# Three tiles of the delta rule under way at once, with each score piece's product, rectification and addition placed slots apart

## What is computed

```
h = rms_norm(x); proj = h @ w_in          # q, k, v, indexer q/k/w, delta-rule q/k/v/z, b, a
# A: sparse attention. For each query t and each key s (chunk-causal):
iscore[t, s] = sum_h w[t, h] * relu(q_idx[t, h] . k_idx[s])      # 8 indexer heads
keep the 256 best keys of every query, softmax attention over them
# B: gated delta rule, chunks of 64, per head
a = I + strict_tril((k * beta) k^T * decay)
u, w = solve(a, [v * beta, k * beta * exp(gc)])
v_new = u - w @ state
o = (q * exp(gc)) @ state + att @ v_new
state = state * g_last + k_tail^T @ v_new
x = x + concat(o_a, rms_norm(o) * silu(z)) @ w_out
x = x + square(relu(rms_norm(x) @ w_ff1)) @ w_ff2 ; rms_norm(x)
```

## Time and profile before

| | us |
|---|---|
| median of 3 runs (lowest, highest) | 4432.31 (4430.19, 4437.88) |
| profiled execution | 4433.13 |
| its span, first to last instruction | 4431.3 |
| mean granted clock of TensorE | 0.894 |

### The profile page before, as it was taken

The page is one execution under the profiler, slowest core; times in us unless marked ns, Lnnn a source line. Parts: engine busy times, 40 slices in busy tenths (PEclk is TensorE's granted clock), DMA queues, the critical chain, the costliest instruction groups (busy, mean ns, idle before and its releaser), DMA issues.

```text
span 4431.3 us, 47714 instructions
## 1 busy us (share of the span) xinstructions
PE 3629.1 (82%) x16994; PEld 2930.3 (66%) x16994; DVE 2057.7 (46%) x3590; ACT 2188.2 (49%) x3674; POOL 1257.9 (28%) x648
## 2 busy tenths in 40 slices
PE   3899997567676666646689998899988899998998
PEld 2688885456555544534567776778776788876886
DVE  3101330466766444435364564756655757543222
ACT  3112222365564333333569768687777684443322
POOL 0110111322322322113234342333332333333442
PEclk7899998787888777776889999999999999999999
DMA  2111123210101111023333334333333333333332
GB/s 72 65 71 66 71 76 95 57 36 22 47 24 38 43 45 30 23 65 103 91 93 108 107 111 128 95 106 118 101 116 116 108 110 106 94 108 105 95 96 75
DMA packets 294561, 358.65 MB, mean 81 GB/s; under 512 B 23361, under 2 KB 234177, under 8 KB 290369
## 3 DMA queue, kind: packets, MB, share of 16 engines
q1 hardware_dynamic: 290464, 327.68, 25.5%
q10 hardware_dynamic: 3888, 28.31, 1.5%
HBM read 297.80 MB, written 58.10 MB: 80 GB/s over the span
## 4 chain that ended last, share of the span: by engine, by line
PE 26%; ACT 14%; DVE 7%; issue 5%; POOL 2%; SPq 1%; DMA 1%; ACTq 0%; DVEq 0%; POOLq 0%
PE m_ps L1823 7%; PE m_ps L1825 7%; PE m_ps L1824 7%; ACT m_junk L1536 6%; ACT m_wh L1593 2%; PE m_ps L1917 1%; PE m_ps L1903 1%; ACT m_prob L1620 1%; ACT m_verdict L1538 1%; ACT m_trial L1542 1%; ACT m_phi L1609 1%; PE m_ps L1888 1%; PE m_ps L1889 1%; PE m_ps L1866 1%; ACT m_rl L1552 1%
## 5 line engine op out<-in xcount | busy, mean ns | idle before, releaser
L1481 POOL TENSOR_TENSOR m_wl<-m_raw,m_wh 128x1024 fp32r<-128x1024 f32 x288 | 716.0, 2486 | 1414.5 <-ACT m_wh L1593 1414.5
L1823 PE MATMUL m_ps<-m_ah,m_wh 128*128 128x512 f32 x1280 | 537.8, 420 | 69.1 <-DVE m_al L1682 40.4
L1825 PE MATMUL m_ps<-m_ah,m_wl 128*128 128x512 f32 x1280 | 512.2, 400 | 0.0
L1824 PE MATMUL m_ps<-m_al,m_wh 128*128 128x512 f32 x1280 | 512.0, 400 | 0.0
L1823 PE MATMUL m_ps<-m_th,m_wh 128*128 128x512 f32 x1024 | 428.4, 418 | 41.6 <-DVE m_tl L1662 25.1
L1825 PE MATMUL m_ps<-m_th,m_wl 128*128 128x512 f32 x1024 | 406.4, 397 | 0.0
L1824 PE MATMUL m_ps<-m_tl,m_wh 128*128 128x512 f32 x1024 | 405.3, 396 | 0.0
L1536 ACT ACTIVATE m_junk<-m_sc,m_trial 128x1152 int8<-128x1152 f32 (+7 forms) x248 | 401.6, 1619 | 1.3
L656 PE MATMUL i_ps<-i_keys,i_qhi 128*128 128x512 f32 (+3 forms) x304 | 171.5, 564 | 264.2 <-ACT i_relu L834 250.9
L1593 ACT ACTIVATE m_wh<-m_raw 128x1024 fp32r<-128x1024 f32 x288 | 302.6, 1051 | 126.8 <-PE m_ps L1825 122.0
L250 PE MATMUL ps<-xh,wh 128*128 128x512 f32 x864 | 337.0, 390 | 12.4 <-POOL wl L126 12.4
(11 more groups left out here) (292 smaller groups left out, 7487.8 us busy)
## 6 DMA issues: line engine op xcount, KB each, us to landing
m_raw<-w_units SPq DMA_DIRECT2D x288, 512.0 KB, 3.7
m_vals<-valsT SPq DMA_DIRECT2D x256, 128.0 KB, 3.7
projT<-stage ACTq DMA_DIRECT2D x15, 1024.0 KB, 3.9
wraw<-w_proj SPq DMA_DIRECT2D x28, 512.0 KB, 3.6
projT<-work ACTq DMA_DIRECT2D x12, 1024.0 KB, 3.9
g_qkvz<-projT SPq DMA_DIRECT2D x16, 768.0 KB, 6.2
work<-xT SPq DMA_DIRECT2D x8, 1024.0 KB, 5.7
i_rot<-projT SPq DMA_DIRECT2D x32, 256.0 KB, 4.5
```

Source lines behind the costliest of these rows:

```text
L1481: nc.gpsimd.tensor_tensor(wl[:, n % 3, :], raw[:, n % 2, :], wh[:, n % 3, :].bitcast(fp32), ALU.subtract).then_inc(w_lo, 1)
L1823: nc.tensor.matmul(dst, hi, rh, start=first, stop=False)
L1824: nc.tensor.matmul(dst, hi, r_low, start=False, stop=False)
L1825: return nc.tensor.matmul(dst, lo, rh, start=False, stop=last)
```

## The change

The back is divided into a middle (b0 to b7) and a tail (b8 to b12). In round r the tail is for tile r - 2, the middle for tile r - 1, and the front for tile r: 18 rounds in place of 16 and a front of its own. The steps of the three parts alternate in a new `ROUND`. Each part has its own counting semaphores, `Z` has two buffers, and each part has two PSUM banks (the middle loses its third, the front too, the tail gets its own two), for which PE waits at some places where a bank's reader comes late. A piece's product is now placed at least one slot behind the rectification whose bank it needs, its rectification at least one slot behind the addition whose buffer it needs, and its addition at least one slot behind its rectification. The diff, cut:

```diff
-ROUND = "b0 f0 b1 f1 b2 f2 b3 f3 b4 b5 f4 b6 f5 b7 f6 b8 b9 f7 b10 b11 b12".split()
+ROUND = "b8 b0 b9 b1 b10 f0 b2 b11 f1 b3 b12 f2 b4 f3 b5 f4 b6 f5 b7 f6 f7".split()
+FRONT, MID, TAIL = range(3)
+PART = {"f%d" % i: FRONT for i in range(8)} | {"b%d" % i: MID if i < 8 else TAIL for i in range(13)}
...
-        end = STAGES * NT
+        end = STAGES * (NT + 2)
...
-                slot = dve(slot, ("acc", j, h, x), 760)
+                slot = dve(slot, None, 760)
...
+                score_slot.append(max(ready, slot - 2, relu_slot[n - 2] + 1 if n >= 2 else 0))
+                relu_slot.append(max(score_slot[n], acc_slot[n - RELUS] + 1 if n >= RELUS else 0))
+                slot = max(slot, relu_slot[n] + 1)
                 acc_slot.append(slot)
-                relu_slot.append(max(ready, slot - 3, acc_slot[n - RELUS] if n >= RELUS else 0))
-                score_slot.append(max(ready, relu_slot[n] - 2, relu_slot[n - 2] if n >= 2 else 0))
...
-        BANK = {n: i % 3 for i, n in enumerate("ssq ssk gb kk att NT atT kT vT n2 m2".split())}
-        BANK |= {n: 3 + i % 3 for i, n in enumerate(
-            "n4 m4 Y1 n8 Y2 Y3 Dinv E F Z1 E2 F2 Z2 E4 Z3 wT vnew out state oss".split())}
+        BANK = {n: i % 2 for i, n in enumerate("ssq ssk gb kk att NT atT kT vT n2 m2".split())}
+        BANK |= {n: 2 + i % 2 for i, n in enumerate("n4 m4 Y1 n8 Y2 Y3 Dinv E F Z1 E2 F2 Z2 E4 Z3".split())}
+        BANK |= {"wT": 4, "vnew": 5, "out": 4, "state": 5, "oss": 5}
...
-            for s in [s for s in ROUND if s[0] == "f"]:
-                front(0, s)
-            for t in range(NT):
+            for r in range(NT + 2):
                 for m, s in enumerate(ROUND):
-                    selection(t, m)
-                    if s[0] == "b":
-                        back(t, s)
-                    elif t + 1 < NT:
-                        front(t + 1, s)
+                    selection(r, m)
+                    t = r - PART[s]
+                    if 0 <= t < NT:
+                        (front if PART[s] == FRONT else back)(t, s)
...
+                if s == "f1":
                     po("G")
+                    ac("ln")
                     over_features("gb", B("G")).then_inc(done_f, 1)
...
                     transposes("atT", B("at")).then_inc(done_f, 1)
-                    transposes("kT", qk[:, 1, :, :]).then_inc(done_f, 1)
                 if s == "f6":
                     dv("LT")
+                    transposes("kT", qk[:, 1, :, :]).then_inc(done_f, 1)
+                    ac("attT")
                     transposes("vT", qkvz[:, t % 2, 2, :, :]).then_inc(done_f, 1)
                 if s == "f7":
                     po("n")
-                    ac("attT")
+                    dv("kbe")
                     heads(0, "n2", B("m"), B("n"))
-                    dv("kbe")
+                    dv("vb")
                     heads(0, "m2", B("n"), B("m"))
...
                     po("Y")
+                    ac("n4")
                     heads(1, "Y1", B("n2"), B("Y"))
...
                     heads(1, "E2", B("F"), B("E"))
+                    dv("Z1")
                     heads(1, "F2", B("E"), B("F"))
```

More of the change, by code:

```diff
@@ L314, in dve @@
             ahead[0] += cost
-            self.put("dve", slot, part)
+            if part:
+                self.put("dve", slot, part)
             return slot
@@ L464, in deltanet_and_selection @@
         stored = [sem(f"g_stored{u}") for u in range(2)]
-        done = {e: [sem(f"g_{e}_{part}") for part in ("front", "back")] for e in ("pe", "dve", "act", "pool")}
+        done = {e: [sem(f"g_{e}_{part}") for part in ("front", "mid", "tail")] for e in ("pe", "dve", "act", "pool")}
         z_in = [sem(f"g_z_in{u}") for u in range(2)]
@@ L551, in selection @@
                         sp.dma_start(biasT[j, :, 0:(j + 1) * P], ties[:, 0:(j + 1) * P]).then_inc(bias_stored, 16)
-            for t in range(NT):
-                if t + 2 < NT:
-                    waits(sp, t, 0)[0]("vT")
-                    waits(sp, t, 0)[1]("qk")
-                    load_tile(t + 2, 0, 3, load)
-                for m in range(STAGES):
-                    selection(t, m)
-                waits(sp, t, 1)[3]("out")
-                sp.dma_start(mixT[4:8, :, tokens(t)].rearrange("c p s -> p c s"), out_b[:, t % 2, :, :]).then_inc(stored[t % 2], 16)
-                if t + 2 < NT:
-                    load_tile(t + 2, 3, 4, z_in)
+            for r in range(NT + 2):
+                if 1 <= r < NT - 1:
+                    waits(sp, r - 1, FRONT)[0]("vT")
+                    waits(sp, r - 1, FRONT)[1]("qk")
+                    load_tile(r + 1, 0, 3, load)
+                for m in range(STAGES):
+                    selection(r, m)
+                t = r - TAIL
+                if t >= 0:
+                    waits(sp, t, TAIL)[3]("out")
+                    sp.dma_start(mixT[4:8, :, tokens(t)].rearrange("c p s -> p c s"), out_b[:, t % 2, :, :]).then_inc(stored[t % 2], 16)
+                    if t + 2 < NT:
+                        load_tile(t + 2, 3, 4, z_in)
             for u in range(2):
@@ L616, in back @@
             def back(t, s):
-                pe, dv, ac, po = waits(pool, t, 1)
-                step = lambda ins: ins.then_inc(done["pool"][1], 1)
+                pe, dv, ac, po = waits(pool, t, PART[s])
+                step = lambda ins: ins.then_inc(done["pool"][PART[s]], 1)
                 if s == "b0":
@@ L873, in back @@
                     pe("out")
+                    if t:
+                        waits(act, t - 1, TAIL)[3]("out")
                     step(nc.scalar.activation(B("osq"), bank("out"), ACT.Square))
```

79 lines of the change are left out of this document (45 added, 34 removed).

## The result

The changed kernel takes 4211.76 us in the median of 4 runs (4209.04 to 4215.33); the kernel before, run beside it on the same chip, takes 4434.94 (4 runs, 4430.19 to 4437.88). The ratio is 0.9503, with a 95% interval of 0.9491 to 0.9515: 223 us less. Forecast were 4223, between 4110 and 4370.

The account below looks back on a forecast made before the run. The second stage was taken as bound by hand-offs, same-slot waits making each slot a sum. Round 0, rounds 1 to 10, 11 to 16 and 17 gave 68 + 498 + 390 + 42 = 998 us against 1207: 4223 us, range 4110 to 4370.

Parts of the forecast that it names:

- rounds 0 and 1: Second stage's start: round 0 with first front, key rotation and first pieces at 68 us, then one early round at 47.
- rounds 2 to 10: Early rounds, DVE fullest: 47 us each, plus 10 for rounds 3 and 7 and 8 for waits on rotated queries.
- round 17: Last round, no front or middle, 30 pieces: 21 slots of two additions and a hand-off, 42 us.
- A late round: Rounds 11 to 16: PE busy 54 us plus 11 of stalls, 65 us each; bounds 57 and 76.
- busy time times granted clock takes the clock out: Step costing PE's late-round work at full clock: 46.8 us, then 54 at clock 0.87.
- What PE still stands for: Late-round PE stalls: rectification wait goes; f1 3 us, f6 and f7 4, b5 and b0 1, POOL effects 3; together 11.
- a sign of "right": Among the signs confirming the forecast: PE's wait for rectifications under 10 us a round.
- Three chains side by side should take from that: Early rounds: three parts under way should cut the 8 to 12 us beyond DVE's busy time; 8 taken, with f1 and f6 waits.
- the fullest engine: Early rounds: DVE, 406 us busy up to round 9, taken as the fullest engine, giving 39 us a round.
- The rounds keep their length: Rival: remaining same-slot waits keep a slot at 4.6 us, with two rounds more: 126 us slower, 4559; 7 in 100.
- The clock rival: Second stage: PE stays at 1.2 GHz, 215 us slower, 4648; 1 in 100.
- a slot is that sum: Late rounds before: a 4.6 us slot sums product, copy or addition, score addition, rectification and score product.

Follow-up runs that it names:

- The placement alone: Kernel before, with its two tiles, three banks and own step order, given only the new placement of pieces: 4199.66 us, ratio 0.9472.
- three tiles alone: Changed kernel with three tiles under way but pieces placed as in the kernel before: 4442.35 us, ratio 1.002.
- the fastest kernel: Changed kernel with square and logarithm steps moved, transposes' banks swapped, and LT awaited a step later: 4157.34 us, ratio 0.9366.
- the even order: Changed kernel with square and logarithm steps moved, and the three parts' steps spread evenly over the round: 4215.08 us, ratio 0.9506.
- narrow pieces: Later tiles' pieces of heads 1 to 7 cut to 8 columns: 4348.99 us from the kernel before, 4173.41 from the changed kernel.
- shorter leads: Kernel before, rectification at most two slots ahead of its addition, product in its rectification's slot if free: 4238.62 us, ratio 0.9565.

## Why the prediction was right, and where not

The reading of the loop was right: its links stood in the same slot, PE's wait was for rectifications, and opening the loop took 222 us from the stage where 209 were forecast. (The placement alone took 236.5.) By terms:

| stretch | forecast | measured |
|---|---|---|
| rounds 0 and 1 | 115 | 127.0 |
| rounds 2 to 10 | 451 | 473.8 |
| rounds 11 to 16 | 390 | 352.5 |
| round 17 | 42 | 31.7 |
| sum | 998 | 985.0 |

The sum is nearer than its terms: two were too low by 35 us together and two too high by 48. That it came within 13 us is in part luck.

*A late round*, forecast at 65 us: rounds 11 to 15 took 305.0 / 5 = 61.0. Its two parts were off in opposite ways. PE's work was forecast at 54 us busy and is 236.87 / 5 = 47.4; the stalls were forecast at 11 and are 13.6. From before, a late round lost 36.5 us: 20.1 of standing (33.6 to 13.6) and 16.4 of busy time (63.8 to 47.4), the latter with four to five pieces fewer and at a clock of 0.89 against 0.77. What failed is "busy time times granted clock takes the clock out". By that product three tiles alone need 235.34 x 0.80 / 4 = 47.1 us a late round at full clock, and the change, with the same pieces, 236.87 x 0.89 / 5 = 42.2. Where PE stood more, the product gave 12% more for the same instructions, and the rows of before that the forecast used (0.87 and 0.77, at 77% and 65% busy) were of that kind. The bounds of this term were summed wrongly: 54 with the f1 and f6 stalls is 61 and not 57, and half of a 35 us wait is 17.5, so 82 and not 76. The measured 61.0 lies at the lower one.

*Round 16* was counted as one of six equal rounds, but it has no front: 47.5 us, not 65. That slip is half of what rounds 11 to 16 were too high. *Round 17* was costed at two additions in each of 21 slots, 42 in all, where the plan has 34 there, and took 31.7.

*What PE still stands for.* The logarithm in f1 was forecast at 3 us a round and took 52.1 / 15 = 3.5; f6 and f7 at 4, where `LT` and `kbe` took (38.5 + 6.9) / 16 = 2.8. The wait for rectifications, said to go, fell to a quarter: 25.4 us in rounds 11 to 15, 5.1 a round, under the 10 that was set as a sign of "right", and 1.6 in round 14 (1545.2 to 1604.8). Not foreseen was f0: PE waits there 57.2 / 16 = 3.6 us a round for ACT's square. The diff leaves the square as it was, but not its place: f0 now stands between b10 and b2. Twelve of these waits, of 0.9 to 3.8 us, come to 26.5 us, about what two tiles have (24.3); what three tiles added lies in the other four. One is of 14.2 us in the first round (3.3 with two tiles), where ACT first waits for DVE's rotation of the keys. The other three are of 4.1, 6.7 and 5.7 us in late rounds, where the new plan puts ACT's rounding of the next tile's queries into f0, ahead of the square, and this waits for POOL's rotation. Round 14:

```profile
1561.61 1.06 ACT L844 ACTIVATE i_qhi<-i_rot 128x1024 fp32r<-128x1024 f32 x1 [4.83 <-POOL i_rot L601]
1562.57 0.74 ACT L851 ACTIVATE i_relu<-i_ps 128x512 f32<-128x512 f32 x2
1563.20 1.06 ACT L858 ACTIVATE g_sq<-g_qkvz 128x1024 f32<-128x1024 f32 x1
```

Moving only that rounding out of f0 was not tried.

*Rounds 2 to 10* were forecast at 451 / 9 = 50.1 us in the mean and took 52.6. The forecast for a round without many pieces was 47 us, 39 of DVE and 8 beside it. The six of these with fewest pieces (2, 5, 6, 8, 9, 10) took 49.3 in the mean, 34.9 of DVE and 14.4 beside it. "Three chains side by side should take from that" is the step that failed: rounds 2, 5 and 8 of before stood 8 to 12 us beside DVE's work, three tiles alone stand 11 to 16 in rounds 5, 6, 8, 9 and 10, and the waits in f0 and f1 come in every round. Nor is DVE "the fullest engine" there: PE is busy 434 us against 406, and 341.92 against 323.47 after. Rounds 5, 6, 9 and 10 took 46.0, 48.1, 53.1 and 48.7 us, where more than 53 was set as a sign of "wrong": only one is above it, by 0.1. Rounds 3 and 7, with pieces, took 62.2 and 63.6, forecast at 57.

*Rounds 0 and 1* took 12 us more: PE waits 24.6 us there for POOL's first rotated queries, at a clock of 0.67; the sum had 8 us for this, counted in rounds 2 to 10.

*The rivals.* "The rounds keep their length" didn't come for the change, but three tiles alone are nearer to it than to the forecast: 90.0 us a late round where it gave 98, though 9 us slower in all and not 126. The forecast gave no share of the gain to either half of the diff, and the third tile brought none. The clock rival fell: the stage rose from 0.80 to 0.85. The Trainium skill (page "TensorE: Matmul & The Clock Gate", section "A second HAM failure mode: psum-queue depth-cycling") has the clock rise and fall where PE stands shortly between groups of products while it goes through banks. On the waits the rows agree in kind: 0.77 in late rounds with 165.0 us of waits for rectifications, 0.89 with 25.4. That fewer banks would bring this on was the prediction's own step, since the page names no number of banks, and the rows show no price of it: 0.85 with two banks and three tiles, 0.86 with three banks and two tiles, and 0.87 with two banks in the fastest kernel. Two banks against three with all else equal was not tried.

*The mechanism's statement* "a slot is that sum" holds as a sum of hand-offs and work, not of the pieces' durations alone: with half of DVE's time for the scores a late round was 83.7 us and not 55.

What stays open: what the banks cost by themselves, whether three tiles bring anything over two once the waits of both are moved, why the even order raises waits on DVE, and how what is left of a late round with narrow pieces divides between hand-offs and instructions.

## What to carry to other kernels

When engines in order share one list of slots, look for a loop through their queues, and count for each link how many slots lie between the part that frees a buffer and the part that needs it: a loop closed in one slot makes the slot a sum, one open link gives back most of it (195 us with shorter leads, 234 with both links open), and placing work as early as allowed is what closed it here. Test the halves of a change one at a time: here the small half (a few lines of a planner) carried everything, and the large one cost 12 us, which went when one wait was moved in both. A PE wait taken away gave back a part of itself: 34 of 43 us and 21 of 24 for the square, 10 of 25 for the logarithm; for `LT`, 11 of 16 by the times and 18 by the ratios, so that what this one gave back isn't known more closely.

## What the runs showed of the hardware

An addition on DVE may take far longer beside POOL's work. In round 15 two of them took 1.41 us while POOL stood and 4.12 beside a rotation on POOL (start, us, engine, line, what):

```profile
1609.27 1.41 DVE L964 SCALAR_TENSOR_TENSOR i_score<-i_relu,i_w,i_score 128x512 f32<-128x512 f32 x2
...
1612.47 2.38 POOL L596 TENSOR_TENSOR i_rot<-i_rot,i_cos 128x1024 f32<-128x1024 f32 x1 [13.74 <-DMA i_rot<-projT]
1613.80 4.12 DVE L964 SCALAR_TENSOR_TENSOR i_score<-i_relu,i_w,i_score 128x512 f32<-128x512 f32 x2
1614.81 2.82 POOL L598 TENSOR_TENSOR i_rot<-i_rot,i_sin 128x1024 f32<-128x1024 f32 x1
```

The timelines of the stage give a price. Additions of 512 columns that overlap work on POOL took about 1.2 us each and the others 0.66, before and after alike; 47% of them overlapped before and 54% after, and the mean of all 266 additions rose from 939 ns to 984. At 8 columns they took about 0.7 us beside POOL's work and 0.2 without: the extra half microsecond is the same.

The granted clock was higher in late rounds where PE stood less: 0.77 before (65% busy), 0.80 with three tiles alone (65%), 0.89 after the change (78%), 0.90 with the placement alone (76%). The busy share doesn't tell it alone: with narrow pieces PE was busy 69% and the clock was 0.71.
